# Two-model transformer block on one Trainium2 core: attention heads kept feature-major, five landing slots that double as lower parts, and an earlier copy of transposed probabilities

## The reference

```python
# first stack, layer l
h = hybrid_mixer(x, ...)          # differential attention (4 heads), neighbourhood attention (8 heads),
                                  # short convolution; gates; w_branch; w_mix_out
x = layer_norm(alpha * x + h, ...)
h = memory_cross_attention(x, mem, ...)    # 4 heads of 256 features
x = layer_norm(alpha * x + h, ...)
h = conv_ffn(x, ...)              # silu(dwconv(gate) + b) * up, D_FF = 2816
x = layer_norm(alpha * x + h, ...)
# second stack, layer l
x = x + 0.5 * swiglu(rms_norm_2(x), ...)
mix = concatenate([y_pool, y_moba, y_dil, y_conv])   # 4 causal heads, 4 dilated causal heads, pooling,
x = x + mix @ w_out[l]                               # a 31-tap convolution with its own layer norm
x = x + 0.5 * swiglu(rms_norm_2(x), ...)
```

## Time and profile before

| what | us |
|---|---|
| three runs | 2282.15, 2287.42, 2293.49 (median 2287.42) |
| the profiled execution's own time | 2269.32 |
| its span, first to last instruction | 2267.5 |
| TensorE matmuls busy | 2138.3 (94%), 17460 instructions |
| VectorE busy | 1436.8 (63%) |
| ScalarE busy | 1009.3 (45%) |
| GpSimd busy | 99.7 (4%) |
| mean granted TensorE clock | 0.974 of full speed |

### The profile page before, as it was taken

One profiled execution on the slowest core, in us unless ns is written; L12 is line 12 of the kernel. 1 busy time (PEld: TensorE's weight loads), 2 busy tenths in 40 slices (PEclk: granted clock), 3 DMA queues, 4 the chain that ended last, 5 costly groups with the idle time before them and its releaser, 6 DMA issues.

```text
span 2267.5 us, 39445 instructions
## 1 busy us (share of the span) xinstructions
PE 2138.3 (94%) x17460; PEld 2080.3 (92%) x17460; DVE 1436.8 (63%) x1690; ACT 1009.3 (45%) x1166; POOL 99.7 (4%) x69
## 2 busy tenths in 40 slices
PE   7999999899899999989997999879999999979998
PEld 6899999899899999989997999769999999868997
DVE  5665554666765656457776756866666666765665
ACT  4544454444445443544444434334444444234443
POOL 1000010100100000010001000001000000000000
PEclk9999999999999999999998999989999999989999
DMA  5444543355444455435552554323554555213542
GB/s 198 148 162 163 204 162 143 133 185 189 149 149 165 146 188 191 152 112 216 186 189 104 199 192 175 112 75 135 204 203 149 209 200 186 112 68 115 209 186 94
DMA packets 52858, 366.08 MB, mean 161 GB/s; under 512 B 5904, under 2 KB 5904, under 8 KB 9296
## 3 DMA queue, kind: packets, MB, share of 16 engines
q1 hardware_dynamic: 52272, 361.21, 43.3%
q0 software_dynamic: 416, 2.35, 0.3%
HBM read 362.49 MB, written 1.05 MB: 160 GB/s over the span
## 4 chain that ended last, share of the span: by engine, by line
PE 76%; DVE 10%; issue 9%; ACT 3%; POOL 1%; DMA 0%; POOLq 0%; ACTq 0%; DVEq 0%
PE accM L989 43%; PE scoreP L989 17%; PE outP L989 8%; PE turnP L989 7%; DVE wlo L1317 2%; DVE yc L1704 1%; ACT whi L728 1%; PE turnP L1176 1%; DVE xl L1335 1%; ACT ew L909 1%; DVE acc L1350 1%; PE outP L1203 0%; DVE cen L1395 0%; DVE cen L1401 0%; DVE mrs L1646 0%
## 5 line engine op out<-in xcount | busy, mean ns | idle before, releaser
L1317 DVE TENSOR_TENSOR wlo<-raw,whi 128x2048 fp32r<-128x2048 f32 x325 | 744.1, 2290 | 411.5 <-ACT whi L728 411.0
L728 ACT ACTIVATE whi<-raw 128x2048 fp32r<-128x2048 f32 x336 | 640.4, 1910 | 256.4 <-PE accM L989 169.9
L989 PE MATMUL accM<-xh,whi 128*128 128x256 f32 x1152 | 338.9, 294 | 16.8 <-DVE xl L1415 10.9
L989 PE MATMUL scoreP<-xh,whi 128*128 128x256 f32 x1152 | 325.9, 283 | 17.8 <-DVE xl L1415 9.0
L989 PE MATMUL accM<-xl,whi 128*128 128x256 f32 x1152 | 324.9, 282 | 0.0
L989 PE MATMUL accM<-xh,wlo 128*128 128x256 f32 x1152 | 324.9, 282 | 0.0
L989 PE MATMUL scoreP<-xl,whi 128*128 128x256 f32 x1152 | 323.7, 281 | 0.0
L989 PE MATMUL scoreP<-xh,wlo 128*128 128x256 f32 x1152 | 323.5, 281 | 0.0
L989 PE MATMUL accM<-fh,whi 128*128 128x256 f32 x1056 | 293.2, 278 | 0.7 <-DVE wlo L1317 0.7
L989 PE MATMUL accM<-fh,wlo 128*128 128x256 f32 x1056 | 293.1, 278 | 0.0
L989 PE MATMUL accM<-fl,whi 128*128 128x256 f32 x1056 | 293.1, 278 | 0.0
(11 more groups left out here) (264 smaller groups left out, 4297.2 us busy)
## 6 DMA issues: line engine op xcount, KB each, us to landing
raw<-in_W SPq DMA_DIRECT2D x336, 1024.0 KB, 4.8
biasr<-in_bias SPq DMA_DIRECT2D x16, 256.0 KB, 2.7
raw<-in_memT SPq DMA_DIRECT2D x2, 1024.0 KB, 4.7
cc<-in_consts POOLq DMA_DIRECT2D x1, 1536.0 KB, 6.7
x<-in_xT SPq DMA_DIRECT2D x4, 256.0 KB, 4.4
out<-x SPq DMA_DIRECT2D x4, 256.0 KB, 2.5
c<-in_consts SPq DMA_DIRECT2D x1, 464.5 KB, 6.1
par<-in_par POOLq DMA_DIRECT2D x2, 203.5 KB, 3.7
```

The source lines that it names most:

```text
L728: nc.scalar.activation(whi[:, slot(c), :], raw[:, n % RING, :], ACT.Copy).then_inc(split_hi.sem, 1)
L989: return nc.tensor.matmul(dst, a, b, start=start, stop=stop, skip_group_check=True)
L1317: v.tensor_tensor(wlo[:, slot(c), :], raw[:, n % RING, :], whi[:, slot(c), :].bitcast(F32), ALU.subtract).then_inc(split_lo.sem, 1)
```

## The change

The heads other than `diff` stay feature-major. The probabilities are divided by their row sum before they are transposed: VectorE does a reciprocal and two `tensor_scalar` in place on `ew` in its part of step `turn`, and signals `evened`; TensorE's transposes wait for that instead of for the exponential. `mix` then takes v as the stationary operand and the transposed probabilities as the moving one, so its result is already feature-major: two heads of 64 features share a bank, one in the upper and one in the lower 64 partitions. The back transposes of these heads, and `otok`, go; `back` is left to ScalarE and VectorE, which read the mix's bank. In the second stack causal heads compute, transpose and multiply 384 instead of 512 columns (`TRI`), and `back` comes one position earlier, behind `mix` in the table.

`raw` and `wlo` now lie at the same addresses, five slots, and the subtraction writes over its input; `whi` has four slots. SyncE therefore loads chunk c when TensorE is done with c-5. ScalarE's split of c waits for TensorE's c-4. The split that stands at position p is that of p+3 (`lead`), at positions that carry `ends` p+2. GpSimd's splits go to VectorE. ScalarE's copy of the transposed probabilities (`turn`) now comes ahead of its split.

```diff
-RING = 3
+RAW_RING = 5
+HI_RING = 4
+LEAD = 3
...
-                    at(pos + 3, "back", h)
+                    at(pos + 2, "back", h)
...
-            order = dict(rot=1, cstats=2, cspread=2, pool=2, back=3, mix=4, turn=5, scores=6, poolw=7, taps=8,
+            order = dict(rot=1, cstats=2, cspread=2, pool=2, mix=3, back=4, turn=5, scores=6, poolw=7, taps=8,
...
-        raw = sb("raw", [P, RING, CH])
-        whi = sb("whi", [P, RING, CH], F32R)
-        wlo = sb("wlo", [P, RING, CH], F32R)
+        landing = ExitStack()
+        raw = sb("raw", [P, RAW_RING, CH], where=landing)
+        landing.close()
+        wlo = sb("wlo", [P, RAW_RING, CH], F32R)
+        whi = sb("whi", [P, HI_RING, CH], F32R)
...
-        by_pool = [c["c"] + 2 for c in chunks if "ends" in c and c["c"] + 2 < len(chunks)]
...
+        def lead(pos):
+
+            return pos + LEAD - 1 if pos < len(chunks) and "ends" in chunks[pos] else pos + LEAD
...
-                if c["c"] >= RING:
-                    await_split(sp, c["c"] - RING)
...
+                if c["c"] >= RAW_RING:
+                    old = chunks[c["c"] - RAW_RING]
+                    if old["kind"] == "M":
+                        await_split(sp, old["c"])
+                    else:
+                        await_chunk(sp, old)
...
-                            "mix", "csquare", "yc", "lam", "cstats", "cspread", "pool", "poolw")
+                            "mix", "turn", "csquare", "yc", "lam", "cstats", "cspread", "pool", "poolw")
...
-                if c["p"] >= RING:
-                    await_chunk(act, products[c["p"] - RING])
...
+                if c["p"] >= HI_RING:
+                    await_chunk(act, products[c["p"] - HI_RING])
...
-                        pe.wait_ge(expd.sem, expd.at(n))
+                        pe.wait_ge(evened.sem, evened.at(n))
...
+                            if kind in ("moba", "dil"):
+                                if k > t:
+                                    continue
+                                at = (k + t) * P
...
+                    if kind == "diff":
+                        bank[mix_bank[n][0]].claim(pe, oscaled, n)
+                    elif kind == "xa":
+                        bank[mix_bank[n][0]].claim(pe, back_lo, n)
+                    elif j % 2 == 0:
+                        bank[mix_bank[n][0]].claim(pe, back_lo, n + 1)
...
+                    elif kind == "xa":
+                        for d in range(2):
+                            for k in range(2):
+                                ins = mm(mix_bank[n][1][:, d * S:(d + 1) * S], v[:, k, v0 + d * P:v0 + (d + 1) * P],
+                                         e[:, k * S:(k + 1) * S], k == 0, k == 1)
+                    else:
+                        rows = slice(64 * (j % 2), 64 * (j % 2) + 64)
+                        late = P if kind != "win" else 0
+                        o = mix_bank[n][1]
+                        mm(o[rows, 0:S], v[:, 0, v0:v0 + w], e[:, 0:S], True, False)
+                        ins = mm(o[rows, late:S], v[:, 1, v0:v0 + w], e[:, S:2 * S - late], False, True)
...
-                mine = [s for s in steps.get(pos, []) if s[0] in PE_STEPS]
+                mine = [s for s in steps.get(pos, []) if s[0] in PE_STEPS
+                        and (s[0] != "back" or s[1]["kind"] == "diff")]
...
-                if n in by_pool:
-                    return
...
-                    split_at(pos + 2)
+                    split_at(lead(pos))
...
+                elif name == "turn" and what["kind"] != "diff":
...
+                    dve.wait_ge(expd.sem, expd.at(n))
...
+                    v.reciprocal(s, rsum[:, i0:i0 + 2]).then_inc(inverted.sem, 1)
+                    dve.wait_ge(inverted.sem, inverted.at(n))
...
+                        e = ew[:, 2 * (j % 2) + t, keys(kind, t)]
+                        last = v.tensor_scalar(e, e, s[:, t:t + 1], None, ALU.mult)
+                    last.then_inc(evened.sem, 1)
```

More of the change, by code:

```diff
@@ L70 @@
 NC0 = _at
-NC2 = 4 * 512 + 512 + 512
+TRI = P + S
+NC2 = 4 * 512 + 2 * TRI
 class Signal:
@@ L299, in kernel_program @@
         att = ExitStack()
-        biasr = sb("biasr", [P, 3, 2, S], where=att)
+        biasr = sb("biasr", [P, 3, 2 * S], where=att)
         qr = sb("qr", [P, 4, S], where=att)
@@ L407, in kernel_program @@
                     turn += 1
-                if name == "mix" and c["kind"] in ("F", "T"):
+                if name == "mix" and what["kind"] not in ("diff", "xa") and what["j"] % 2:
+                    mix_bank[what["n"]] = mix_bank[what["n"] - 1]
+                elif name == "mix" and c["kind"] in ("F", "T"):
                     mix_bank[what["n"]] = (f"acc{turn % 4}", accM[:, turn % 4, :])
@@ L425, in kernel_program @@
         cs = [c["c"] for c in chunks]
[L426 removed]
+        landed = [sem(f"landed{i}") for i in range(RAW_RING)]
         split_hi = sig("split_hi", cs)
[L429 to L431 removed]
+        split_lo = sig("split_lo", cs)
         def await_split(engine, c):
[L434 to L435 removed]
+            engine.wait_ge(split_lo.sem, split_lo.at(c))
         used = sig("used", [c["c"] for c in products if "ends" not in c])
@@ L506, in kernel_program @@
             for name, what, *_ in steps.get(c["c"], []):
-                if (name == "scores" and what["kind"] == "diff") or (name == "mix" and what["kind"] != "diff"):
+                if (name == "scores" and what["kind"] == "diff") or (name == "turn" and what["kind"] != "diff"):
                     inverse_order.append(what["n"])
@@ L517, in kernel_program @@
         mixed = sig("mixed", stage["mix"])
-        oscaled = sig("oscaled", stage["mix"])
+        oscaled = sig("oscaled", [n for n in stage["mix"] if hs[n]["kind"] == "diff"])
         o2 = sig("o2", [n for n in stage["mix"] if hs[n]["kind"] == "diff"])
@@ L521, in kernel_program @@
         oroot = sig("oroot", [n for n in stage["mix"] if hs[n]["kind"] == "diff"])
-        backed = sig("backed", stage["back"])
+        backed = sig("backed", [n for n in stage["back"] if hs[n]["kind"] == "diff"])
         back_hi = sig("back_hi", stage["back"])
@@ L1200, in step @@
                     pe.wait_ge(oscaled.sem, oscaled.at(n))
-                    for d in range(2 if kind == "xa" else 1):
-                        for t in range(2):
-                            ins = nc.tensor.transpose(outP[:, d * S + t * P:d * S + (t + 1) * P],
-                                                      otok[:, t, d * P:(d + 1) * P], ident)
+                    for t in range(2):
+                        ins = nc.tensor.transpose(outP[:, t * P:(t + 1) * P], otok[:, t, 0:P], ident)
                     ins.then_inc(backed.sem, 1)
@@ L1247, in needs @@
                 if c["role"] == "wo":
-                    return (name, what["kind"] if name == "back" else "") in {
-                        0: [("poolw", "")], 1: [("back", "moba")], 2: [("back", "dil")], 3: [("cspread", "")]}[c["j"]]
-                return c["role"] == "xo" and name == "back" and what["j"] == c["j"]
+                    return (name, what["kind"] if name == "mix" else "") in {
+                        0: [("poolw", "")], 1: [("mix", "moba")], 2: [("mix", "dil")], 3: [("cspread", "")]}[c["j"]]
+                return c["role"] == "xo" and name == "mix" and what["j"] == c["j"]
             hooks = {}
@@ L1693, in step @@
                     else:
-                        v.tensor_tensor(lo, outP[:, 0:S], hi.bitcast(F32), ALU.subtract).then_inc(back_lo.sem, 1)
+                        v.tensor_tensor(lo, mix_bank[n][1][:, 0:S], hi.bitcast(F32), ALU.subtract)\
+                            .then_inc(back_lo.sem, 1)
                 elif name == "trig":
@@ L1887, in layout @@
     bias = table[:, np.where(ok, dr * 31 + dc, 15 * 31)]
-    out["bias"] = np.ascontiguousarray(bias.reshape(DEPTH * 8, 2, P, S).transpose(0, 2, 1, 3))
+    out["bias"] = np.ascontiguousarray(bias.reshape(DEPTH * 8, 2, P, S).transpose(0, 2, 1, 3).reshape(DEPTH * 8, P, -1))
     out["W"] = weight_chunks(i, products)
```

156 lines of the change are left out of this document (81 added, 75 removed).

## The result

| | before | changed |
|---|---|---|
| median (range) of the runs compared, us | 2284.78 (2262.66 to 2293.49) | 2336.11 (2317.01 to 2339.23) |
| profiled execution, us | 2269.32 | 2333.79 |
| its span, us | 2267.5 | 2332.0 |
| mean granted TensorE clock | 0.974 | 0.968 |

The ratio is 1.0263 with a 95% interval of 1.0218 to 1.0308: 51 us between the medians, 64.5 us between the two profiled executions. The forecast was 2315, the range 2268 to 2348; it started from 2287.42, the median of the three runs then known.

A forecast was written before the change was run, and what follows sets the result against it. TensorE's matmuls bound the feed-forward stretches; gain and loss sit where TensorE waits. -20 - 1 - 1.8 + 17.8 + 5.4 + 13 + 14 = +27.4 us on the 2287.42 median gave 2315, range 2268 to 2348.

The forecast's parts named there:

- The window loop: Window heads: transposes wait for VectorE's scaling, a loop through three engines once a position; +17.8 us, bounds 0 and 2 x 14.
- Work taken off TensorE: Window heads: sixteen back transposes at 0.11 us go and the mix stays level; -1.8 us.
- Differential heads: Differential heads: ScalarE's copy ahead of its split makes VectorE 0.9 us late at three positions; +5.4 us, bounds 0 and 8.
- Memory heads: Memory heads, positions 48 to 55: transposes and a mix wait for VectorE; 6.4 us, twice, +13, bounds -2 and 20.
- GpSimd's splits: Norms: VectorE no longer held by GpSimd; -20 us, 7.0 of it at four layer norms, 12.1 at five RMS norms.
- TensorE has nothing to do there: Layer norm at 400 us: TensorE idle while VectorE's sum is held, so 1.76 us returns at each of four norms.
- Deeper rings: Loading and split: one 1.0 us wait for `wlo` beside the trigonometric steps goes; -1 us.
- The second stack: Second stack's heads: splits and taps delay transposes at 220, partly regained from 222 to 225; +7 a layer, +14 us.
- my rival of the layers that recover: Second stack: later positions recover the first transposes' delay, the layer gains 10; sum -7, 2281, no change; chance 0.18.
- Rate: Feed-forward stretches of 33 chunks keep one of two rates; each turning is worth 7 us either way, widening the range about 12.

The follow-up runs named there:

- the other bank: Changed kernel with the mix of memory head 3 in bank scoreP0 instead of outP: 2315.89 us, one execution.
- the rings alone: Kernel before with the memory edits only (rings of five and four, split three ahead, GpSimd's splits on VectorE), heads untouched: 2274.42 against 2276.26, ratio 0.998.
- copy ahead only: Kernel before with ScalarE's copy eT ahead of its split, no scaling ahead of the transposes: 2297.25 us, ratio 1.0094.
- layer norms' splits on VectorE: Kernel before with the splits behind the six layer norms moved to VectorE, those behind RMS norms still on GpSimd: one execution, 2298.14 us.
- the copy behind: Changed kernel with ScalarE's copy eT put back behind its weights' split: 2280.05 us, ratio 1.0014.
- first stack early: Changed kernel, copy behind its split, first stack's scaling one position earlier, head 3's mix in scoreP0, split two positions ahead: 2257.29 us, ratio 0.9934.
- scale ahead of the split: Best version: changed kernel with copy behind its split, head 3's mix in scoreP0, split two positions ahead, scaling before VectorE's split, second convolution two positions later: 2239.54, ratio 0.9866.
- split two ahead: Changed kernel with the split two positions ahead everywhere, rings of five and four kept: one execution, 2302.63 us.

## Why the prediction was right, and where it was wrong

**The window loop** was right in mechanism and place, and 6 us too small in size: 22.0 us of stall against 17.8 - 1.8. Position by position (forecast, measured in the first layer): 13: 0.7, 1.4; 16: 3.8, 5.0; 18: 1.9, 1.6; 19: 2.0, 2.7. That either end of the loop, opened, takes away half of it or more shows it. Not in the forecast were 0.3 us each at 14, 15 and 17.

**Work taken off TensorE** was mis-sized. I priced a head's mix at 0.85 us, the window scores' row less its tail, against 0.81 before. But the 0.81 goes from the mix's first start to the next product's, and the row less its tail leaves that last distance out (0.31 us behind the scores). Start to start it now takes 1.01 us, for 4 matmuls of 256 columns instead of 8 of 64:

```profile
140.06 1.08 PE L1012 MATMUL accM<-eT,vb 128*64 128x256 f32 x4
```

Its matmuls start 0.21 to 0.27 us apart, the next product 0.31 behind the last: 16.1 us for sixteen heads instead of 12.9. That is +3.2, and the transposes that go, which I had at 1.8, took 1.1 by starts. The quiet positions 14, 15 and 17 are each 0.3 us longer. In the best version these three and 1.3 us at position 19, less 0.6 at 20, are the 1.6 us by which the window heads stay above before.

**Differential heads**: 6.1 against 5.4, and the copy's place alone accounts for all of it.

**Memory heads**: 17.4 against 13. Forecast and measured: 48: 1.5, 1.5; 50: 2.4, 2.9; 52: 0.8, 1.0. The missed size is position 54: 2.2 forecast, 4.9 measured, of which 3.7 went with the other bank. I had VectorE reach `ol` 2.7 us in; its split, held by ScalarE's, put it later.

**GpSimd's splits** were half wrong. The held-up instructions are as the rows had them: without GpSimd's subtractions `acc` takes 0.69 us and a pair of `xl` 0.87. This agrees with what the Trainium skill ("SBUF — State Buffer", Who interferes with whom) states, an exclusive lock. At the RMS norms the 12.1 us came (14.2 measured, 13.0 with the rings alone). The failed step is "TensorE has nothing to do there", said of the layer norms: it had sixteen sums of `x`, 3.75 us, and the 7.8 us were 0. I read VectorE's and GpSimd's rows at the norm and not TensorE's.

**Deeper rings**: the 1 us beside the trigonometric steps can't be put down to them. Position 189 is 0.9 us shorter, but so it is in two kernels that keep three slots (copy ahead only, layer norms' splits on VectorE), and the four with deep rings and the split two ahead have the stall of before. And 1.2 us were lost at the first down product of each of four feed-forwards. That two splits follow each other behind `ends` was in `lead`, and I counted it at 214 (+2.2; measured +2.0 at 216, partly given back by 218) but not in front of `fp`.

**The second stack** is where the sum was near for a wrong reason, by luck: +14 forecast, +18.1 measured, 13.5 without the clock of the profile before. The wait of 12 us stood where I put it. But the runs show that about half of it is given back: with the wait (first stack early) the second stack ends 4.1 and 6.0 us above the version without it (scale ahead of the split). So far my rival of the layers that recover held: with the copy behind, the heads end at +1.7 and -2.6 in spite of the wait. What costs is ScalarE's copy, which takes the exponentials ahead of the split with it: 9.7 and 9.3 us between the changed kernel and the one with the copy behind. The prediction had seen the split behind the exponentials, but priced it at 3 us of delay at 220 alone, and then counted 12 us back from 222 to 225. The changed kernel got back 4.6 and 5.9 there, with the copy behind 9.9 and 11.4. The term that failed is that saving: it holds only with the copy behind.

**Rate**: +9.9 us in this execution, which I had put outside the forecast and inside the range. Without it, 54 us, near the 51 of the medians. Of the 37 us that the profile stands above my sum, 10 are rate, 15 heads under-priced, 8 the layer norms, 6 the catching up, less 2 at the RMS norms; 4.6 of the 15 are the clock of the profile before.

## What to carry to other kernels

When a wait is added between engines, follow it round until it closes: here transposes, copy, split, split, scaling, transposes. It costs little while one link stands ahead of the long work and a lot when none does, so test the corners one at a time. A step belongs where its engine would wait anyway. Putting the copy back, the scaling a position earlier, one bank and the catching-up split took the stall from +54 to -13 us against before; the scaling in front of the split, while ScalarE still splits, and one convolution moved took it on to -27. Together they turned +2.6% into -1.3%.

A held-up instruction is a gain only if the engine that ends the stretch is idle for it. Read that engine's rows at the same place before the saving is booked. And a long wait on the list is not a loss of its own length: 12 us stood at position 220 in a version whose stretch ended level with before, and taking them away was worth 4 to 6. A single profile of the kernel before is a baseline with a luck of its own: where it has the same stretch twice, compare the two first.

## What the runs showed of the hardware

TensorE's products have two rates at the same granted clock. The stretch of the feed-forward (positions 59 to 88), in the kernel before and in the changed one:

```profile
420.00:600.00 180.00, 180.00 (x1517) 180.00 (x1516) 122.28 (x132) 85.60 (x80) 2.59 (x2) 0.99 0.49 180
```
```profile
445.00:620.00 175.00, 175.00 (x1544) 175.00 (x1543) 127.00 (x135) 86.31 (x77) 1.30 (x1) 1.00 0.53 189
```

TensorE is busy throughout both. Start to start a matmul takes 0.1178 us at these positions in the first, 0.1133 in the second; the first window's clock of 0.99 comes from its first microseconds, from 440 us on it is 1.00 too. That stretch ran at the slower rate in the kernel before and in two of the eleven others, and 6.4 us quicker in nine; other stretches turned the other way. Over a whole execution the rate moved the profiles between -15 us (split two ahead) and +22 us (layer norms' splits on VectorE) against before. A stretch keeps its rate until a stall; in the twelve profiles the only turns from one to the other with no stall on either side lie between positions 44 and 45 and between 134 and 135, where a value projection of the memory attention (`xv`) is followed by a query projection (`xq`). What picks the rate stays open, so a profile's total should be read by stalls, and small differences by medians.

At the lower level of the clock the same products start 0.21 us apart. How many do so behind a wait differs between executions and layers: position 220 of the kernel before had 7 such distances in the first layer and its counterpart 299 had 25 in the second, with the same 4.9 and 4.8 us of waits. So one and the same wait can cost 4 us more or less behind it.
